# First projections of a transformer kernel with the input part as the outer loop, and scale, shift and weight rows streamed part by part

## The reference, cut to what matters

```python
shift, scale, gate = jnp.split((c @ mod_w[0, 0] + mod_b[0, 0])[:, None, :], 3, axis=-1)
h = rms_norm(x, norm_w[0, 0, 0]) * (1.0 + scale) + shift
proj = h @ w_in_ab                     # 1024 features -> 2072 columns
...                                    # two attention mixers on slices of proj
y = jnp.concatenate([o_a, o_b], axis=-1) @ w_out_ab
x = x + gate * rms_norm(y, norm_w[0, 0, 1])
```

## Time and profile before

| what | value |
|---|---|
| time, median of 3 runs | 1223.87 us (1223.73 to 1225.53) |
| the profiled execution's own time | 1224.81 us |
| its span, first to last instruction | 1223.0 us |
| TensorE matmul busy | 1141.5 us (93%) |
| VectorE busy | 948.4 us (78%) |
| ScalarE busy | 602.7 us (49%) |
| GpSimd busy | 77.7 us (6%) |
| chain that ended last, by engine | PE 64%, DVE 22%, ACT 6%, DMA 6% |

### The profile page before, as it was taken

How to read it: one execution, slowest core, us unless ns; L and a number is a source line. 1 busy time by engine, 2 the same in 40 slices (tenths; PEclk the granted TensorE clock), 3 DMA queues, 4 the chain that set the end, 5 groups by cost and what they waited for, 6 DMA issues and landing times.

```text
span 1223.0 us, 19512 instructions
## 1 busy us (share of the span) xinstructions
PE 1141.5 (93%) x8036; PEld 1022.7 (84%) x8036; DVE 948.4 (78%) x1638; ACT 602.7 (49%) x1055; POOL 77.7 (6%) x110
## 2 busy tenths in 40 slices
PE   2699889899999989999999999999999979999996
PEld 1588579899997987898998899999979967888885
DVE  5998768888868965788888778887776867777655
ACT  2445854434356466644435663443453265555553
POOL 1030000000000000383000000000000000000000
PEclk9999999899999999999999999999999999999998
DMA  9986427787973942377798438799732542666731
GB/s 374 359 306 251 159 83 277 308 308 224 398 292 114 411 152 82 124 262 300 291 266 341 189 139 322 288 258 356 286 117 110 83 180 96 227 248 259 186 121 35
DMA packets 41098, 280.74 MB, mean 230 GB/s; under 512 B 4769, under 2 KB 5297, under 8 KB 8241
## 3 DMA queue, kind: packets, MB, share of 16 engines
q1 hardware_dynamic: 37584, 269.27, 60.6%
q0 software_dynamic: 2416, 7.92, 2.0%
q10 hardware_dynamic: 1008, 2.30, 0.6%
HBM read 277.85 MB, written 1.10 MB: 228 GB/s over the span
## 4 chain that ended last, share of the span: by engine, by line
PE 64%; DVE 22%; ACT 6%; DMA 6%; issue 2%; SPq 0%; DVEq 0%; ACTq 0%
PE PS L421 63%; DVE LO L1465 8%; DMA raw<-WS 6%; DVE raw L1455 5%; ACT HI L1006 3%; DVE TMP L1534 1%; DVE HB L1529 1%; ACT SC L1006 1%; DVE TMP L1807 1%; ACT SQ L1006 1%; PE PS L644 1%; DVE TMP L1571 1%; ACT HB L1006 1%; DVE X L1576 1%; DVE FB L1653 1%
## 5 line engine op out<-in xcount | busy, mean ns | idle before, releaser
L421 PE MATMUL PS<-HB,HI 128*128 128x256 f32 (+1 forms) x3160 | 651.3, 298 | 30.4 <-ACT HB L1006 18.6
L421 PEld LDWEIGHTS PS<-HB,HI 128*128 128x128 f32 x3160 | 511.0, 192 | 60.2 <-ACT HB L1006 21.1
L421 PE MATMUL PS<-HB,LO 128*128 128x256 f32 x1748 | 494.7, 283 | 0.0
L1465 DVE TENSOR_TENSOR LO<-raw,HI 128x1024 fp32r<-128x1024 f32 x340 | 406.5, 1233 | 90.1 <-ACT HI L1006 90.1
L1006 ACT ACTIVATE HI<-raw 128x1024 fp32r<-128x1024 f32 x340 | 339.2, 1049 | 96.5 <-DMA raw<-WS 51.5
L421 PEld LDWEIGHTS PS<-HB,LO 128*128 128x128 f32 x1748 | 335.5, 192 | 2.8
L1455 DVE CUSTOM_DVE_ANT_0 raw<-raw,CB,SM 128x1024 f32<-128x1024 f32 x168 | 211.9, 1296 | 15.8 <-DMA raw<-WS 15.5
L1006 ACT ACTIVATE HDH<-FB 128x256 fp32r<-128x256 f32 x88 | 37.0, 420 | 231.0 <-DVE FB L1653 207.3
L421 PE MATMUL PS<-HI,HDH 128*128 128x512 f32 x352 | 140.2, 398 | 0.0
L421 PE MATMUL PS<-HI,HDL 128*128 128x512 f32 x352 | 139.4, 396 | 0.0
L421 PE MATMUL PS<-LO,HDH 128*128 128x512 f32 x352 | 139.1, 395 | 0.0
(11 more groups left out here) (234 smaller groups left out, 916.7 us busy)
## 6 DMA issues: line engine op xcount, KB each, us to landing
raw<-WS SPq DMA_DIRECT2D x255, 1024.0 KB, 5.2
SC<-scratch POOLq DMA_DIRECT2D x2, 1024.0 KB, 16.0
FB<-gates_out POOLq DMA_DIRECT2D x3, 512.0 KB, 5.4
SQ<-gates_out POOLq DMA_DIRECT2D x3, 512.0 KB, 10.0
X<-xT ACTq DMA_DIRECT2D x1, 1024.0 KB, 6.8
SC<-ssm POOLq DMA_DIRECT2D x2, 512.0 KB, 3.8
out<-TMP SPq DMA_DIRECT2D x4, 256.0 KB, 2.6
CB<-vecs SPq DMA_DIRECT2D x1, 512.0 KB, 6.4
```

The costliest lines, as they stand in the source:

```text
L421: return e.matmul(o, l, r, start=start, stop=stop, skip_group_check=True)
L1465: e.tensor_tensor(LO[:, s % HL, :], raw_half(j, h), HI[:, s % HL, :].bitcast(fp32), O.subtract).then_inc(*D.up(("lo", s)))
```

## The change

Mod chunk k (k below 8) now holds the scale column and the shift column of feature part k. The chunks `ab` 0 to 3 hold input rows 256n to 256n+255 for all eight output tiles, not two tiles for all rows. The stream goes mod, mod, ab 0, mod, mod, ab 1, and so on, then ab 7; all twelve later mods come behind it, one to three in a step of the attention loop. Eight accumulators stay open in the four work banks, and k is the outer loop on TensorE. VectorE makes the row roots first and then goes part by part. The first bias DMA waits until part 4 is made, the second for the end of the values, and `firsts` is loaded with 33 rows, not 128.

```diff
-    plan = mods(0, 4)
+    plan = []
     am = mods(4, 6)
-    plan += weave([("w", ("ab", i)) for i in (0, 1, 2, 3, 7)], am[:6], 0)
+    for i in range(4):
+        plan += mods(i, 1) + [("w", ("ab", i))]
+    plan += [("w", ("ab", 7))]
     third = [("w", ("ab", i)) for i in (4, 5, 6)]
-    plan += [third[0], am[6], ("raw", ("cmp", 0)), am[7], third[1], am[8], third[2]] + am[9:] + ws("abo", 4)
+    plan += [third[0], am[0], ("raw", ("cmp", 0)), am[1], third[1], am[2], am[3], third[2]] + am[4:] + ws("abo", 4)
...
-            for n in range(4):
-                linear_fm(("ab", n), H2, "ab", 8, 2)
-            values_only(("ab", 7))
+            ps = [take(("first", b)) for b in range(4)]
+            for k in range(8):
+                key, half = ("ab", k // 2), k % 2
+                wt = [x.rearrange("p (t n) -> p t n", t=8) for x in weight(key, half)]
+                for t in range(8):
+                    i = mm3(ps[t // 2][:, t % 2 * 256:t % 2 * 256 + 256], [x[:, t, :] for x in wt], H2[k], k,
+                            k == 0 and t % 2 == 0, k == 7, "ab")
...
-            low(walk.catch_up(walk.at_unit[3, 1]))
             roots("ab")
-            low(walk.catch_up(walk.at_unit[7, 1]))
-            factors("ab", 8, S("nw")[:, 0:8], 0)
-            modulate("ab", 0)
...
+            w.wait_ge(*A.at(("free", ("rb", "ab", 1))))
+            for k in range(8):
+                low(walk.catch_up(walk.at_unit[mod_at[k], 1]))
...
+                if k:
+                    first_low(k - 1)
+                if k % 2:
+                    for half in range(2):
+                        use(("ab", k // 2), half, 0)
+            first_low(7)
...
-                low(walk.spare(2))
+                low(walk.spare(2 if p < 4 else 3))
                 for f in compressed.get(p, ()):
                     f()
-                if 6 < p:
-                    low(walk.catch_up(walk.unit - 1, 1))
+                if p == 6:
+                    gate("f0", 16, -0.5, S("nw")[:, 8:16])
+                if p == 8:
+                    low(walk.weight(("abo", 0), 0, 0))
...
             w.wait_ge(*TABOUT.at(1))
+            w.wait_ge(*D.at(("hlo", "ab", 4)))
             skewed(0)
-            skewed(1)
...
+            w.wait_ge(*A.at(("fm", "ab")))
+            skewed(1)
```

More of the change, by code:

```diff
@@ L206, in build, with mod_col @@
     order = {u: n for n, u in enumerate(u for u in units if plan[u[0]][0] == "w")}
+    mod_at = {p[1]: i for i, p in enumerate(plan) if p[0] == "mod"}
+    def mod_col(m, t):
+        return (m if t else 8 + m) if m < 8 else 2 * m + t
     ctx = ExitStack()
@@ L543, in modulate @@
             def modulate(tag, sc, fill=(0, 0, 0, 0)):
-                mods(sc + 8)
                 if tag != "ab":
+                    mods(sc + 8)
                     busy_wide(fill[0])
@@ L699, in pe @@
                 banks.give(("tab", q))
-            walk.catch_up(walk.at_unit[4, 1])
             w.wait_ge(*G.at("consts"))
             modulate("ab", 8)
-            for n in range(4):
-                linear_fm(("ab", n), H2, "ab", 8, 2)
-            values_only(("ab", 7))
+            ps = [take(("first", b)) for b in range(4)]
[5 more added lines that the diff above has]
+                            k == 0 and t % 2 == 0, k == 7, "ab")
+                    if t == 7 or (k == 7 and t % 2):
+                        i.then_inc(*P.up(*([("first", t // 2)] if k == 7 else []), *([used(key, half)] if t == 7 else [])))
+            for b in range(4):
+                banks.give(("first", b))
+            for half in range(2):
+                wt = [x.rearrange("p (k n) -> p k n", k=4) for x in weight(("ab", 7), half)]
+                linear_tm(lambda qt: PS[:, 0, qt * 256:qt * 256 + 256], ("ab", 7), half, range(4 * half, 4 * half + 4), wt,
+                          half == 0, half == 1)
             def third_set(p):
@@ L1184, in act @@
             e.dma_start(X[:, :, :], xT).then_inc(*XIN.up("in", by=16))
-            e.dma_start(SC[:, 10752:10752 + fw], firsts).then_inc(*FIRST.up("in", by=16))
+            e.dma_start(SC[0:33, 10752:10752 + fw], firsts).then_inc(*FIRST.up("in", by=16))
             e.dma_start(CN[:, :], consts).then_inc(*CONST.up("in", by=16))
             e.preload_act_table_set(LNEXP)
-            high(walk.catch_up(walk.at_unit[3, 1]))
-            w.wait_ge(*SMALL.at("in"))
+            roots("ab")
+            spread("ab")
             for q in range(2):
@@ L1192, in act @@
                 fn(vbs[q], bank(("tab", q))[0:8, 0:384], F.Copy).then_inc(*A.up(("free", ("tab", q))))
[L1193 to L1196, removed]
+            for k in range(8):
+                high(walk.catch_up(walk.at_unit[mod_at[k], 1]))
+                if k % 2:
+                    for half in range(2):
+                        use(("ab", k // 2), half, 0)
+                w.wait_ge(*D.at(("tmp", "ab", k)))
+                fn(HH[:, k, :], TMP[:, k, :], F.Identity, bias=MV[:, k:k + 1]).then_inc(*A.up(("hh", "ab", k)))
             fn(HDH[:, 0, 0:192], S("gate"), F.Copy).then_inc(*A.up("gatew"))
+            use(("ab", 7), 0, 2)
+            use(("ab", 7), 1, 2)
             for n, i in enumerate((4, 5, 0, 1)):
-                use(("ab", n), 0)
-                use(("ab", n), 1)
-                evacuate(("ab", n), flat(FMT[:, 2 * i:2 * i + 2, :]), ("proj", "ab", n), 0.125 if i < 4 else 1.0)
+                w.wait_ge(*P.at(("first", n)))
+                fn(flat(FMT[:, 2 * i:2 * i + 2, :]), bank(("first", n)), F.Copy, scale=0.125 if i < 4 else 1.0) \
+                    .then_inc(*A.up(("proj", "ab", n), ("free", ("first", n))))
                 if n == 0:
@@ L1209, in act @@
                                 .then_inc(*DUPED.up("in", by=16))
-            use(("ab", 7), 0, 2)
-            use(("ab", 7), 1, 2)
-            values(("ab", 7), 0, ("fm", "ab"))
+            w.wait_ge(*P.at(("lin", ("ab", 7), 1)))
+            fn(VT[:, :, 0:256], PS[:, 0, :].rearrange("p (q n) -> p q n", q=2), F.Copy).then_inc(*A.up(("fm", "ab")))
             def third_set(p):
@@ L1698, in biased @@
                 w.wait_ge(*P.at(("s", tag, i)))
-                w.wait_ge(*SKEW.at("bias"))
+                w.wait_ge(*SKEW[bh // 8].at("bias"))
                 w.wait_ge(*G.at("consts"))
@@ L1710, in biased, with first_low @@
                     e.tensor_tensor(ex, S("sink")[:, h0:h0 + nh], m, O.add).then_inc(*D.up(("m", tag, i)))
-            low(walk.catch_up(walk.at_unit[3, 1]))
             roots("ab")
-            low(walk.catch_up(walk.at_unit[7, 1]))
-            factors("ab", 8, S("nw")[:, 0:8], 0)
-            modulate("ab", 0)
+            w.wait_ge(*SMALL.at("in"))
             e.tensor_scalar(nsink, S("sink"), -1.0, None, O.mult).then_inc(*D.up())
+            def first_low(k):
+                w.wait_ge(*A.at(("hh", "ab", k)))
+                e.scalar_tensor_tensor(HLo[:, k, :], TMP[:, k, :], MV[:, k:k + 1], HH[:, k, :].bitcast(fp32), O.add,
+                                       O.subtract).then_inc(*D.up(("hlo", "ab", k)))
+            w.wait_ge(*A.at(("free", ("rb", "ab", 1))))
+            for k in range(8):
+                low(walk.catch_up(walk.at_unit[mod_at[k], 1]))
+                w.wait_ge(*D.now())
+                e.scalar_tensor_tensor(AV[:, k:k + 1], MV[:, 8 + k:9 + k], 1.0, S("nw")[:, k:k + 1], O.add, O.mult) \
+                    .then_inc(*D.up())
+                w.wait_ge(*D.now())
+                e.scalar_tensor_tensor(TMP[:, k, :], turned(k), AV[:, k:k + 1], RS[:, 3, :], O.mult, O.mult) \
+                    .then_inc(*D.up(("tmp", "ab", k)))
+                if k:
+                    first_low(k - 1)
+                if k % 2:
+                    for half in range(2):
+                        use(("ab", k // 2), half, 0)
+            first_low(7)
             w.wait_ge(*A.at("gatew"))
@@ L2210, in restart @@
             banks.restart()
[L2211 removed]
+            for t in (P, A, D, G, *IN, SMALL, XIN, CIN, C2IN, FIN, ROWOUT, ROWIN, FIRST, CONST, TABOUT, *SKEW, DUPED, SSMIN, OUT):
                 t.n = 0
@@ L2246, in shape_constants @@
     fo, fw = offsets(first_items())
-    out, first = np.zeros((128, cw), np.float32), np.zeros((128, fw), np.float32)
+    out, first = np.zeros((128, cw), np.float32), np.zeros((33, fw), np.float32)
     def put(n, a):
@@ L2320 @@
             m, cs = {"ab": (ab, abc), "cd": (cd, cdc), "in2": (in2, i2c)}[key[0]]
+            if key[0] == "ab" and key[1] < 4:
+                WS[j] = fm(m[key[1] * 256:key[1] * 256 + 256][:, np.concatenate(cs)[:1024]])
+                continue
             a = m[:, np.concatenate(cs)[key[1] * 256:key[1] * 256 + 256]]
```

21 lines of the change are left out of this document (10 added, 11 removed).

## The result

| what | before | changed |
|---|---|---|
| time, median of 5 runs each on one chip | 1225.53 us | 1230.06 us (1228.88 to 1230.67) |
| ratio, 95% interval | | 1.0048 (1.0034 to 1.0062) |
| span of the profiled execution | 1223.0 us | 1228.2 us |
| first bias of the attention loop | 79.85 us | 70.23 us |
| `out_parts` | 142.64 us | 148.86 us |

The changed kernel is slower by 0.5%, and the predicted 1229.2 us lies 0.9 from the median. The loop begins 9.6 us earlier and lasts 15.8 us longer (78.6 against 62.8). The stages answer to the earlier trace rows: start, first projections, VectorE's hole behind them, the loop. The columns are length, then busy time of PE, PEld, DVE, ACT and POOL with instructions, clock, DMA share and GB/s.

A forecast was written before the change was run, and what follows sets the result against it. VectorE, in order with 7.6 us of room, was taken to bound the attention loop. Terms 0.3 + 1.8 + 2.2 + 1.0 = 5.3 us on 1224.81 gave 1230.1; that execution lying 0.94 above the median, 1229.2 us, range 1218 to 1236.

The forecast's parts named there:

- Start of the new chain: Before the first projections: VectorE waits for the spread roots and starts its gemvs at 17.9, 5.5 us later than before.
- A pair of parts: In the first projections: a pair of parts takes VectorE 9.3 us, and VectorE, not DMA, sets the pace.
- TensorE behind it: End of the first projections: last burst at full rate, TensorE done at 68.2, step 0 begins at 70.1 us, 9.7 earlier.
- The hole: Ahead of the loop, from 55 to 70 us: VectorE waits for TensorE and loses some 10 us.
- The loop's work: Attention loop: twelve more gemvs make VectorE's work 69.7 us, 70.5 with small gaps; waits of steps 3 and 5 are absorbed.
- The wait of step 2 and the clock, +2.2: Step 2 of the attention loop: VectorE's 2.3 us wait stays, and TensorE's low clock adds 2.2 (bounds 0 and 2.7).
- GpSimd on top, +1.8: Step 0: GpSimd's additions, 67.7 to 76.2, slow VectorE's two-input work, one by 1.0, one by 0.8 (bounds nothing and 3.5).
- Costed at nothing: `ab` 6 behind the compression chunk: Step 3: `ab` 6 lands some 5 us later, about when wanted; late by 2 it would cost 2.
- The clock at the end, +1.0: Before `scaled` (8): TensorE's low clock lasts up to 6 us, before 2.9, costing 1.0 (bounds 0 and 3).
- even trade: Rival, 1224.2 us, chance 0.22: GpSimd's additions fall into VectorE's wait, step 2's clock holds, only +0.3 is left.
- Every burst at low clock: Rival, 1231.8 us, chance 0.13: in the first projections all four pairs begin cold, the last matmuls end 2.6 later.
- The loop hides it: Rival, 1219.5 us, chance 0.15: ScalarE or TensorE paces steps 6 to 8, hiding eight extra gemvs, 9.7 us.

The follow-up runs named there:

- the cut gemvs: Changed kernel with twelve gemvs of the last six mods ahead of the output projection cut to 32 of 1024 inputs: ratio 1.0007, `out_parts` at 140.33.
- the ordered stream: Changed kernel with four mods ahead of `ab` 4, both its HI halves made before the loop, and chunks reordered: ratio 0.9974, `out_parts` at 140.30.
- the early start: Changed kernel with VectorE's first two gemvs ahead of the wait for the spread roots: ratio 1.0025, `out_parts` at 146.36.
- fillers behind parts 1 to 6: Changed kernel with eight small matmuls of zeros added behind each of parts 1 to 6: ratio 1.0048, `out_parts` at 147.42.
- The later compression chunk: Changed kernel with the compression chunk one place later in the stream, behind the next mod: ratio 1.0017, `out_parts` at 144.96.
- the ordered kernel with the early start: Changed kernel with four mods ahead of `ab` 4, reordered chunks, early HI halves, and two gemvs before the roots wait: ratio 0.9957, `out_parts` at 138.47.

## Why the prediction was right

The forecast and its direction were right, and the mechanism named as the question, twelve gemvs given to an engine without room for them, is what the cut gemvs show (12.3 us of work out, the loop 8.8 us shorter), and the ordered stream bears it out. But that its sum came so near was luck in part: errors of both signs cancel. Step by step:

- **Start of the new chain.** Said 17.9, measured 16.35. The tables started at 9.30 and the transposes at 11.96, some 0.4 sooner than said. The two spread products and the two copies ran almost as one: from the first product at 15.39 to the gemv are 0.96 us, where 0.75 + 1.1 stood in the sum.
- **A pair of parts.** Said 9.3; the LO rows stand at 22.99, 32.29, 41.60 and 50.90: 9.30 each. VectorE, not DMA, set the pace.
- **TensorE behind it.** "The last at full rate" is the step that failed: the clock fell to 0.50 in the last part. It cost 1.5 us (67.74 against 66.27 above), which ate the early start; so the first bias stood at 70.23, where 70.1 was said. The picture of bursts of 5.8 us and waits of 3.5 was wrong too: they were bursts of 2.9 and waits of 1.1 to 1.8. Nor does the length of a wait tell here when the clock falls: behind the same 1.76 us it fell in one kernel's trace and held in another's.
- **The hole.** Said some 10 us, measured 11.72. The ordered stream puts 9.6 us of gemvs there, which gains 4.7 in `out_parts` over the run with only the compression chunk moved.
- **The loop's work.** Said 69.7 and small gaps of 0.8; measured 69.71, and 1.2 of gaps (78.63 - 69.71 - 3.95 - 2.51 - 1.25). The waits of steps 3 and 5 as they were before were taken up, as said, but for 1.25 us of the second.
- **The wait of step 2 and the clock, +2.2.** Said 2.3 + 2.2 = 4.5, measured 3.95. TensorE waited 2.58 us for the LO, not some 4. Where the clock held (fillers behind parts 1 to 6) VectorE's wait was 2.46, so the clock took 1.5 and not 2.2.
- **GpSimd on top, +1.8.** Measured nothing: the additions fell on the wait and the biases, the lower bound. The copies landed 5.7 us after their issue, not 7.6, and the additions took 5.19, not 8.49. With the first bias 1.3 us earlier the charge came, 0.5 + 1.0. The Trainium skill (GPSIMD Engine Reference, Specifications) has VectorE instructions with two SBUF inputs pay for shared interfaces; the traces agree on both sides: LO 1.22 to 1.73, gemv 1.28 to 2.28, a PSUM bias 0.48 with and without.
- **Costed at nothing: `ab` 6 behind the compression chunk.** "Late by 2 it would cost 2" was the text; it was late by 2.51 and TensorE passed 1.25 more on at the end of step 5. The later compression chunk won 3.9 in `out_parts`, 3.5 of it in the loop. This is the largest error of the sum, made by taking the cheap end of a risk that was named.
- **The clock at the end, +1.0.** The output projection took 35.58 us against 35.10: 0.5.

Together: 5.3 foreseen; start -1.55, clock of the last part +1.5, GpSimd -1.8, step 2 -0.55, gaps +0.4, `ab` 6 +3.75, end -0.5: some 6.5. (Of the bounds that it gives, 1226.4 to 1233, the lower does not follow from its terms: with GpSimd and both clock terms at nothing the sum is 0.3 and the time 1224.2.) The first part of the next sublayer was 6.7 us late, and the runs 4.5 (medians) to 5.9 us (ratio). Later stages give some of it back and take it again (+5.7 at 387 us, +7.2 at 508, +5.2 at 1030, at the first input part of each); that scatter was not followed up.

Of the rivals, the **even trade** had its first condition (no charge from GpSimd) but not the second, the clock in step 2. **Every burst at low clock**: only the first (0.50 from 24 to 28 us) and the last were; none of the waits between the bursts reached the 3.1 us of its condition. The Trainium skill (TensorE: Matmul & The Clock Gate, HAM oscillation) tells of bursts between data waits that begin throttled each time; here parts of 2.9 us with waits of 1.1 to 1.8 between them ran at 1.00 from 30 to 52 us, and only the last fell (in the ordered kernel with the early start one at 40 us fell too). The waits in the page's case are longer, and no run here shows a train of such. **The loop hides it** is refuted by the cut gemvs.

## What to carry to other kernels

When a change takes work from ahead of a loop into it, look for the idle time that it leaves on the engine that bounds the loop, and move independent work there; the order of a hand-written stream must then be looked at again as a whole, since each chunk's issue waits for the use of another. Any chunk that is released late by another engine holds back all that stand behind it in an in-order queue: price such a wait, don't name it and cost it at nothing. Where an edit does two things, time each alone before one is given the gain: of the ordered stream's 8.6 us some 4 were the order's. And a gain ahead of a stage is worth only what the next wait leaves of it: 1.3 to 1.5 us of TensorE's time gave nothing twice.

## What was not expected of the hardware

The output projection, the same instructions in each kernel, took 34.06 to 36.82 us (39.98 with the cut gemvs, where it waited for its chunks), and longer the lower its mean clock was. Its windows (columns as in the stages above) in the ordered kernel with the early start, the changed kernel, and the early start alone:

```profile
138.47:172.53 34.06, 31.63 (x154) 24.15 (x152) 22.71 (x43) 19.12 (x39) 0.00 (x0) 1.00 0.56 222
```

```profile
148.86:184.44 35.58, 33.16 (x155) 25.17 (x153) 22.71 (x42) 19.28 (x39) 0.00 (x0) 0.96 0.55 216
```

```profile
146.36:183.18 36.82, 34.40 (x155) 25.93 (x153) 22.79 (x43) 19.29 (x39) 0.00 (x0) 0.92 0.52 204
```

TensorE's busy time moves with the clock, 31.63 at 1.00 and 34.40 at 0.92, VectorE's does not. Waits of TensorE around `scaled` (8) that hardly differ go with it: 4.93 and then 3.49 us in the changed kernel, 4.93 and then 3.67 in the early start; in the ordered kernel, which kept the clock, they are shorter, 3.53 and then 1.29. Why one stretch keeps the clock and the other not was not settled. So a difference of 1 to 1.5 us between the traces of two of these kernels can be the clock of this one stage, of the last part of the first projections or of step 2, and need not be the edit.
